# Last layer norm of a decoder block: one more row tile scaled on ScalarE and stored by an adding DMA

## The reference, cut to what matters

```
def layer_norm(x, g, b):
    mu = jnp.mean(xf, axis=-1, keepdims=True)
    var = jnp.mean(jnp.square(xf - mu), axis=-1, keepdims=True)
    y = (xf - mu) * lax.rsqrt(var + LN_EPS) * g + b
...
    moe = hier_moe(x, w_group[l], b_group[l], w_expert[l], b_expert[l], w_gate[l], w_up[l], w_down[l])
    x = layer_norm(DEEPNORM_ALPHA * x + moe, ln2_g[l], ln2_b[l])
```

## Time and profile before

| | us |
|---|---|
| median of 3 executions | 615.74 |
| lowest and highest | 615.7 and 617.25 |
| the profiled execution, its own time | 615.53 |
| its span, from the first to the last instruction | 613.6 |

### The profile page before, as it was taken

How to read it: one execution, slowest core, us unless ns; L and a number is a source line. 1 busy time by engine, 2 the same in 40 slices (tenths; PEclk the granted TensorE clock), 3 DMA queues, 4 the chain that set the end, 5 groups by cost and what they waited for, 6 DMA issues and landing times.

```text
span 613.6 us, 9635 instructions
## 1 busy us (share of the span) xinstructions
PE 591.4 (96%) x3627; PEld 475.8 (78%) x3627; DVE 478.5 (78%) x572; ACT 373.4 (61%) x401; POOL 129.3 (21%) x111
## 2 busy tenths in 40 slices
PE   8999999999999999999799999999999999999991
PEld 6878888888788668877588888888888888888880
DVE  3748598794577775546898989888888988888967
ACT  3659434431315984213478877877877787787745
POOL 0004222290000340000484443111110111111010
PEclk9999999999999999999899999999999999999997
DMA  9821133223306003975699999999999999999754
GB/s 325 299 98 57 63 130 111 95 71 78 72 1 206 2 2 125 422 271 211 239 375 420 404 363 389 392 388 391 409 404 389 389 389 389 399 410 397 269 172 137
DMA packets 42573, 155.77 MB, mean 254 GB/s; under 512 B 11955, under 2 KB 12163, under 8 KB 30252
## 3 DMA queue, kind: packets, MB, share of 16 engines
q1 hardware_dynamic: 37516, 138.40, 57.8%
q0 software_dynamic: 5024, 16.92, 10.6%
HBM read 139.96 MB, written 15.34 MB: 253 GB/s over the span
## 4 chain that ended last, share of the span: by engine, by line
PE 92%; DVE 4%; issue 1%; ACT 1%; DMA 1%; DVEq 0%; SPq 0%
PE psum L673 26%; PE psum L675 25%; PE psum L674 25%; PE psum L1072 2%; PE psum L791 2%; PE psum L931 2%; PE psum L908 2%; PE psum L1089 1%; PE psum L895 1%; PE psum L687 1%; DMA cst<-in_c_main 1%; PE psum L833 1%; PE psum L821 1%; PE psum L777 1%; DVE ring L2033 1%
## 5 line engine op out<-in xcount | busy, mean ns | idle before, releaser
L1810 DVE TENSOR_TENSOR w_lo<-ring,w_hi 128x2048 fp32r<-128x2048 f32 x95 | 216.8, 2299 | 23.3 <-ACT w_hi L1380 22.1
L673 PE MATMUL psum<-w_hi,act_hi 128*128 128x512 f32 x538 | 216.5, 402 | 0.8 <-DVE w_lo L1810 0.6
L675 PE MATMUL psum<-w_hi,act_lo 128*128 128x512 f32 x538 | 210.3, 391 | 0.0
L674 PE MATMUL psum<-w_lo,act_hi 128*128 128x512 f32 x538 | 210.0, 390 | 0.0
L1380 ACT ACTIVATE w_hi<-ring 128x2048 fp32r<-128x2048 f32 x96 | 182.2, 1917 | 25.0 <-PE psum L675 22.3
L673 PEld LDWEIGHTS psum<-w_hi,act_hi 128*128 128x128 f32 x538 | 101.3, 188 | 26.9 <-DVE w_lo L1810 4.7
L675 PEld LDWEIGHTS psum<-w_hi,act_lo 128*128 128x128 f32 x538 | 101.0, 188 | 21.9
L674 PEld LDWEIGHTS psum<-w_lo,act_hi 128*128 128x128 f32 x538 | 101.2, 188 | 19.0
L627 POOL DMA_INDIRECT acc_dram<-misc,slots x15 | 25.8, 1720 | 192.8 <-ACT misc L1430 178.8
L1228 ACT ACTIVATE w_hi<-ring 128x2048 fp32r<-128x2048 f32 x17 | 32.6, 1918 | 49.0 <-PE psum L675 47.3
L1539 DVE TENSOR_TENSOR w_lo<-ring,w_hi 128x2048 fp32r<-128x2048 f32 x17 | 39.8, 2344 | 23.0 <-ACT w_hi L1228 22.8
(11 more groups left out here) (254 smaller groups left out, 692.7 us busy)
## 6 DMA issues: line engine op xcount, KB each, us to landing
ring<-in_w_gate SPq DMA_DIRECT2D x32, 1024.0 KB, 19.8
ring<-in_w_up SPq DMA_DIRECT2D x32, 1024.0 KB, 19.6
ring<-in_w_down SPq DMA_DIRECT2D x32, 1024.0 KB, 19.9
ring<-in_w_in SPq DMA_DIRECT2D x13, 1024.0 KB
ring<-in_w_o SPq DMA_DIRECT2D x4, 1024.0 KB
acc_dram<-ring SPq DMA_DIRECT2D x5, 512.0 KB, 4.0
ring<-in_x SPq DMA_DIRECT2D x2, 1024.0 KB, 6.4
ring<-strip_dram SPq DMA_DIRECT2D x8, 256.0 KB, 4.9
```

Source lines behind the costliest of these rows:

```text
L673: pe.matmul(dst, lh, rh, start=first, stop=False, skip_group_check=True)
L674: pe.matmul(dst, lh, rl, start=False, stop=False, skip_group_check=True)
L675: return pe.matmul(dst, ll, rh, start=False, stop=last, skip_group_check=True)
L1810: dve.tensor_tensor(w_lo[:, v0 % WBUF, :], ring[:, slot, :], w_hi[:, v0 % WBUF, :].bitcast(F32), ALU.subtract).then_inc(s_lo, 1)
```

## The change

Tile 1 is now treated as tile 0 was. ScalarE scales it (`scaled(1)`), VectorE's `finished(1)` is gone, SyncE stores the bias onto the rows of tile 1 too, and GpSimd issues a second adding DMA in place of SyncE's plain store. On ScalarE the squares of tile 2 move ahead of `scaled(0)`. The semaphore counts follow.

```
             sp.wait_ge(s_lnw, 96)
-            sp.dma_start(out[0:P, :], f_b).then_inc(s_lnw, 16)
+            for i in range(2):
+                sp.dma_start(out[i * P:(i + 1) * P, :], f_b).then_inc(s_lnw, 16)
...
-            for i in range(1, T - 1):
-                sp.wait_ge(s_x1, T - 1 + i)
-                sp.dma_start(out[i * P:(i + 1) * P, :], f_out[:, i, :]).then_inc(s_out, 16)
+            sp.wait_ge(s_x1, T)
+            sp.dma_start(out[2 * P:3 * P, :], f_out[:, 2, :]).then_inc(s_out, 16)
...
-            sp.wait_ge(s_out, 16 * T)
-            sp.wait_ge(s_outadd, 16)
+            sp.wait_ge(s_out, 16 * (T - 1))
+            sp.wait_ge(s_outadd, 32)
...
-            pool.wait_ge(s_lnw, 112)
-            pool.wait_ge(s_x1n, 1)
-            pool.dma_start(out[0:P, :], f_out[:, 0, :], accum_op=ALU.add).then_inc(s_outadd, 16)
+            pool.wait_ge(s_lnw, 128)
+            for i in range(2):
+                pool.wait_ge(s_x1n, i + 1)
+                pool.dma_start(out[i * P:(i + 1) * P, :], f_out[:, i, :], accum_op=ALU.add).then_inc(s_outadd, 16)
...
-            spread(0)
-            spread(1)
+            for i in range(T - 1):
+                spread(i)
             scaled(0)
-            spread(2)
+            scaled(1)
             last_mean()
             spread(T - 1)
...
             gained(2)
-            finished(1)
             inverse(2)
             finished(2)
```

## The result

| | before | after |
|---|---|---|
| median of 9 executions each, us | 616.88 | 619.42 |
| lowest and highest | 615.7, 618.61 | 618.16, 620.43 |
| profiled execution, its time and span | 615.53, 613.6 | 618.16, 616.3 |

The account below looks back on a forecast made before the run. The prediction took the gapless queue of output stores on the DMA engines as the bound: 615.53 + 0.2 (later start) + 1.1 (tile 1 adding) = 616.8, and 0.2 for the median gave 617.0 us, range 615.2 to 618.5.

Parts of the forecast that it names:

- What bounds the kernel: End of the last norm: a gapless queue of output stores on the 16 DMA engines sets the end, not VectorE.
- VectorE's 0.84 us: VectorE's last halves of tile 3 come 0.84 us earlier, which gains nothing behind the DMA backlog.
- ScalarE's and VectorE's steps: Last norm: forecast start times, such as ScalarE's first scaling at 602.74 and VectorE's halves of tile 3 at 608.0.
- The order on ScalarE: Squares of tile 2 ahead of tile 0's scaling: tile 0's adding DMA is issued 0.20 us later, +0.2.
- the bias store: Second bias store, 512 KB at about 580.1: falls where the DMA engines are idle, 0.
- The sign: Whole kernel: slower, by +1.3 us, inside the 0.3% that a measurement can tell.
- the term for the DMA queue: Tile 1's adding transfer takes 2.4 us where its plain store took 1.33: +1.1 us.
- the stretch from the last packet to the program's end: Program's end: 0.7 us in which the last completion is counted; the sum has no term for it.
- The sum: Profiled execution plus two DMA queue terms: 615.53 + 0.2 + 1.1 = 616.8 us.
- Rival B: DMA queue from 609 on: second adding transfer starts slowly or mixes with tile 2's store; +2.1 to +4.1 us; chance 18%.
- rival A: Program's end: the last store's latency sets it, so VectorE's 0.84 us is gained, 614.9 us; chance 12%.
- The formula of the Trainium skill: Tile 3's last half: about 2.0 us plus bytes at 436 GB/s, landing 2.6 us after issue, with no queueing.

Follow-up runs that it names:

- experiment 3: Changed kernel, but tile 1 scaled by ScalarE is stored plainly by SyncE without the bias, one bias store; ratio 1.0002 to the kernel before.
- experiment 4: Changed order on ScalarE and VectorE, but tiles 0 and 1 stored plainly by SyncE, no adding DMA, no bias store; ratio 0.9962 to the kernel before.
- experiment 5: Kernel before with only the squares of tile 2 moved ahead of tile 0's scaling on ScalarE; ratio 1.0003.
- experiment 6: Kernel before with only the second bias store added, overwritten later by tile 1's plain store; ratio 1.0008.
- experiment 2: Changed kernel with all five output stores issued by GpSimd on one queue, none by SyncE; ratio 1.0071 to the kernel before.
- experiment 7: Kernel before with tile 0's adding DMA cut into four of 128x256, the same bytes; ratio 1.0032.
- experiment 8: Kernel before with only the last half of tile 3 issued by GpSimd instead of SyncE; ratio 1.0032.

## Why the prediction was wrong

**Right.** What bounds the kernel: the stores' queue on the 16 DMA engines, with VectorE's 0.84 us lost behind it (experiments 3 and 4; measured 0.85). ScalarE's and VectorE's steps, each within 0.05 us. The order on ScalarE at +0.2 (experiment 5), the bias store at about nothing (experiment 6). The sign: later, not earlier.

**The steps that failed** are two: the term for the DMA queue, +1.1 us, was too small, and the stretch from the last packet to the program's end, which the sum put at nothing, grew. The sum had +1.3 us; the profiled executions differ by 2.63. Read from the DMA packets:

- Tile 0's adding transfer is through at 609.34 instead of 609.11: +0.2, as in the sum.
- From there to the last packet: 5.7 us (to 615.03) instead of 3.8 (to 612.90): +1.9, against +1.1.
- From the last packet to the end: 1.24 us instead of 0.74: +0.5, against nothing in the sum.

0.2 + 1.9 + 0.5 = 2.6.

*The queue.* The prediction divided 128 packets by 53.3 in a microsecond and got 2.4 us. But the earlier trace rows give a share of 110.3%, which says that the 96 packets had 1.99 us of work and not 1.8. At the 331 to 341 ns of one packet on one engine (alone, in turns, and on one queue, where 94 packets in 2.0 us fill 100.2%), 128 packets need 2.65 to 2.7 us of the 16 engines. A plain tile takes 1.27 us (128 packets of 159 ns), not 1.33. So the adding costs +1.4, not +1.1. In the second profile of the changed kernel that is all: 5.27 us from the end of tile 0 to the last packet, +1.5. The first profile has 0.4 us more: 0.1 for plain packets that take 173 ns beside adding ones, and the rest where the engines ended 0.85 us apart instead of 0.2. That the turns caused this is not shown; the kernel of experiment 6 ended ragged without any.

*The end.* The prediction took the stretch behind the last packet as fixed. It is so only while GpSimd's DRAIN is over before SyncE is: the change moved the last packet of GpSimd's queue from 4.5 us ahead of the end to 2.5, and with it the DRAIN became the bound (the rows of the DRAIN, experiments 2, 7 and 8). Here the turns do count. An adding transfer that shares the engines with tile 2's plain store is through later, at 613.7; without the turns it would be at about 609.3 + 2.7 = 612.0, the DRAIN would be over at 614.3, and SyncE's last packet plus 0.7 would be the bound again. That is an estimate.

Rival B, at 18%, was the nearest: it named the place and a mix with tile 2's store, and priced it at +2.1 us or more. Its sign came, queue 0 at 33 packets in a microsecond after 609, but not its mechanism: the adding packets kept their pace, and plain ones passed between them. It did not have the end of the program. That stretch stood in the earlier trace rows as 0.7 us and was explained in the prediction as counting the last completion. The trace of before did hold the other bound, in a row that the prediction did not read: GpSimd's DRAIN, over only at 611.35. Experiment 3 decides against rival A. The formula of the Trainium skill that it quotes is, by the title of its section, one for DMAs that GpSimd issues, while tile 3's halves were SyncE's.

The range, 615.2 to 618.5, missed the median 619.42 by 0.9 us. 1.1 us of the distance to the point forecast is that the nine executions of the kernel before have a median 1.1 us above the three that were shown.

**Open:** what GpSimd's DRAIN waits for in the 2.2 to 2.4 us behind its queue's last packet; why single packets of an adding transfer take up to 1.8 us, and with them why the engines end apart.

## What to carry to other kernels

When the last work of a kernel is stores, read the DMA share ahead of the chain of waits: if it is full from the first output byte on, an engine that gets earlier gives nothing, and an adding store costs at least double: 2.7 us a tile here against 1.3 for a plain one, and 3.3 when it was the first on idle engines. When you read a rate from a stretch, read the share beside it: a share above 1 means that the work does not fit the stretch. Let a kernel's last stores not be GpSimd's, and look at when its DRAIN ends: an adding store that shares the engines with plain ones is through later, and the program's end moves with it.

## What the runs showed of the hardware

- The program ended 2.5 to 2.6 us behind the last packet of a DMA that GpSimd issued (the changed kernel in both its profiles, and four others), adding or plain, and otherwise 0.7 to 0.8 us behind SyncE's last packet. The end is the later of the two. GpSimd's DRAIN ended 2.2 to 2.4 us behind its queue's last packet.
- A 4 KB packet of an adding store took 331 ns on one DMA engine alone and 335 ns in turns with a plain store; a plain one took 159 ns alone and 173 beside it. Two plain queues side by side kept 388 GB/s.
- In one profile five packets of an adding store took 1.8 us each, and the engines ended that store 2.5 us apart.
- The same adding store cut into four of 1 KB rows lengthened the tail by 1.8 us.
- A GpSimd addition of 128x1024 float32 beside VectorE's operations on the same kind of tile: 3.2 us each, and 3.2 to 3.4 us instead of 1.28 for VectorE's.
